# Moving splits, copies and one bank in a three-layer transformer kernel: four edits to the order of work on VectorE and ScalarE

## The chip, the cores and the metric

One core of a Trainium2 chip. The metric is the time on the device, in microseconds (us), of one execution of the whole program. The engines are called by the profile's names: PE is TensorE (PEld its weight loads), DVE is VectorE, ACT is ScalarE, POOL is GpSimd, SP is SyncE, which here only issues DMAs.

## The reference

For 256 tokens of width 2048, in fp32, three blocks follow each other. The first two are attention layers, the third is a mixer with a feed-forward net.

```python
# layer one (MLA): 16 heads, compressed queries and keys, rope on 64 dims, causal softmax
h = rmsnorm(x, layer_norm[0]); c_q, c_kv, k_rope, gate = split(h @ mla_w_in)
q = rmsnorm(c_q, q_norm) @ w_uq;  kv = rmsnorm(c_kv, kv_norm) @ w_ukv
x = x + (attention(q, kv, rope) * silu(gate)) @ mla_w_out
# layer two (SWA): 32 query heads, 4 key heads, window 128, a sink logit per head
q, k, v, gate = split(rmsnorm(x, layer_norm[1]) @ swa_w_in)
p = exp(s - m) / (sum(exp(s - m)) + exp(sink - m))
x = rmsnorm(x + (p @ v * silu(gate)) @ swa_w_out, final_norm)
# layer three: 8 attention heads with a relative bias beside a Mamba-2 mixer with 16 heads
q, k, v, z, xbc, dt = split(rms_norm(x, ln_mix_pre) @ w_in)
xbc = silu(causal_conv4(xbc));  dt = softplus(dt + dt_bias)
mixed = concat(softmax(q k / sqrt(128) + bias) @ v, gated_norm(ssd(xbc, dt), z)) @ w_out
x = x + rms_norm(mixed, ln_mix_post)
u = causal_conv3(rms_norm(x, ln_ffn_pre) @ w_ffn_up)
x = x + rms_norm((gelu(u_gate) * u_up) @ w_ffn_down, ln_ffn_post)
```

## The kernel before

All weights pass through PE once, 512 KB at a time, in "tiles" numbered through the whole program (`T_C`, `T_KR`, `T_MLA`, `T_MLAO`, `T_KV`, `T_SWA`, `T_SWAO`, `T_XBC`, `T_DT`, `T_MOBA`, `T_OUT`, `T_UP`, `T_DOWN`). A product of fp32 numbers is made from three matmuls: each operand is split into a high part (rounded to the type fp32r) and a low part (what the rounding left), and high x high, high x low and low x high are added up in PSUM. Activations come as such pairs too (`hTh`/`hTl`, `cTh`/`cTl`, `yTh`/`yTl`).

So each weight tile has four steps. SP loads it into one of 4 slots, once the low part of the tile 4 earlier is made (lines 414 to 422). ACT casts it to `w_high` (`split`, line 1171), once it has landed and PE is through with the tile 4 earlier. DVE makes `w_low` (`split`, line 1667). PE waits for the low part (`ready`) and does its matmuls: `block_b` (lines 506 to 508), 256 columns each with the weights loaded, or `block_a` (lines 514 to 516). On ACT and DVE the call `split(T + j)` works on tile `T + j + 3`, that is three tiles ahead (`LEAD = 3`).

There is no scheduler: the order on each engine is written out by hand. Between the splits stand the other steps of the layer, and every engine goes through its list in order, waiting on semaphores. `after(engine, sem, n)` waits until the semaphore has passed n. In the steps below `project` says that a step computes the next heads' projections, `attend` that it does the attention of the heads before.

- Layer one, start. `first_gate` computes the first gate tile by tile into bank 0, PE then computes the first queries into banks 0 and 1 in `mla_step(0, True, False)`. Before that it waits for `ml["gate"]`, which `gate_out(0)` on DVE (line 1844) gives when it has read bank 0. `gate_out` needs the tanh of `gate_tanh` on ACT (line 1308), before which a function table is loaded. `scores` is the name of banks 4 and 5; the shared rotary key was in bank 4.
- Layer two, `swa_step`. Five steps, the first without attention, the last (after the loop) with tiles of the out projection. Each attending step treats four head pairs m = 0 to 3: PE makes scores, DVE takes the maxima (line 1711) and their negatives (line 1732), ACT the exponentials (lines 1244, 1246) and that of the sink (line 1394), DVE adds it and scales the rows (`normalised`, lines 1740 to 1745), PE transposes them (line 544), ACT and DVE copy the two halves out (`pt0`, `pt1`, line 1751), PE multiplies with the values (`swa_values`), DVE gates the result (`out_`, line 1838) and POOL splits it (lines 2473, 2474). Sixteen weight tiles run between these. ACT also places the next queries (`qs`, line 1429), which need DVE's rope (lines 1995 to 1999).
- Layer three, before `moba_step`. `xbc_step` projects the input of the convolution and treats it one part late; the last part, `conv_begin(3, 0)` and so on, comes behind the tile `T_DT`. On DVE follow the dt chain (lines 2169 to 2175, with exponentials and a table load on ACT), the copy for the bias (line 2177), and then the first split of `moba_step`. In the first of those steps ACT also writes eight parts of the residual (line 1507) and copies the transposed rows out of PSUM (`xs_out`, line 1520), which PE's `ssm_cb` waits for.
- Layer three, the last `moba_step(4, False, True)`. PE goes through tiles of the out projection; DVE copies `pt1` behind tiles 2 and 3, and copies the attention rows from bank 7 (line 2286) behind tile 6; PE's `ssm_turned` needs bank 7 free for its last four transposes, and its tile 6 needs POOL's split of those rows.

Of the kernel before, what the change touches and what calls it, by code (L numbers as in the profile page):

```python
# [28 lines left out]
ACT = mybir.ActivationFunctionType  # L29
# [146 lines left out]
def after(eng, sem, count):  # L176

    eng.wait_ge(sem, count + 1)
# [23 lines left out]
def program(nc, a, out, toeplitz):  # L202
# [9 lines left out]
    with ctx:  # L212
# [283 lines left out]
        def _(pe):  # L496
# [137 lines left out]
            def first_gate(j):  # L634
                tile_b(T_MLA + j, [banks[0][:, 0:SEQ], banks[0][:, SEQ:2 * SEQ]], range(4 * j, 4 * j + 4), 256,
                       hTh, hTl, 0, DC - 1)
# [18 lines left out]
            def mla_step(i, project, attend):  # L655
# [21 lines left out]
                if project:  # L677
                    after(pe, ml["gate"], 1 if gated_first else i)
                    after(pe, ml["q_rope"], i)
# [478 lines left out]
        def _(act):  # L1158
# [145 lines left out]

            def gate_tanh(used):

                act.wait_ge(tiles_used, used)
                nc.scalar.activation(gtan[:, 0:2, :], banks[0].rearrange("p (h n) -> p h n", h=2), ACT.Tanh,
                                     scale=0.5).then_inc(ml["tanh"], 1)

            split(T_MLA + 2)
            split(T_MLA + 3)
            gate_tanh(T_MLA + 4)
            act.wait_ge(kr_done, 1)
# [69 lines left out]
            def swa_step(i, project, attend):  # L1384
                def tile(*js):

                    for j in js:
                        split(T_SWA + j, i, 16)
# [16 lines left out]
                if project:  # L1405
                    tile(1, 2, 3)
                    pt0(0)
                    tile(4)
                    exps(1)
                    tile(5)  # L1410
                    if not attend:
                        keys_placed()
                    tile(6, 7)
                    pt0(1)
                    tile(8)
                    act.wait_ge(tiles_used, T_SWA + 8 + i * 16)
                    after(act, sw["q_rope"], i)
                    for k in range(2):
                        last = nc.scalar.copy(qsr[:, 2 * k:2 * k + 2, :], banks[k].rearrange("p (h n) -> p h n", h=2))
                    last.then_inc(sw["q_out"], 1)  # L1420
                    exps(2)
                    tile(9, 10, 11)
                    pt0(2)
                    tile(12)
                    exps(3)

                    after(act, sw["s_ready"], 4 * i)
                    after(act, sw["q_rope"], i + 1)
                    nc.scalar.copy(qs[:, :, :], qs_next[:, :, :]).then_inc(sw["q_placed"], 1)
                    tile(13, 14, 15)  # L1430
                    pt0(3)
                    return
# [51 lines left out]
            split(T_DT)  # L1484
            conv_begin(3, 0)
            conv_tanh(3, 0)

            act.wait_ge(sm["dt_x"], 1)
# [5 lines left out]
            def moba_step(i, project, attend):  # L1494
                def tile(*js):

                    for j in js:
                        if project or j < 15:
                            split(T_MOBA + j, i, 16)
                        if project and not attend and j < 8:  # L1500
                            row_of_residual(j)
# [152 lines left out]
        def _(dve):  # L1654
# [184 lines left out]

            def gate_out(i):  # L1840

                after(dve, ml["tanh"], i + 1)
                after(dve, ml["y32_done"], i)
                v.scalar_tensor_tensor(gate[:, 0:2, :], gtan[:, 0:2, :], 1.0,
                                       banks[0].rearrange("p (h n) -> p h n", h=2),
                                       ALU.add, ALU.mult).then_inc(ml["gate"], 1)

            split(T_MLA + 2)
            split(T_MLA + 3)
            gate_out(0)  # L1850

# [112 lines left out]
            def swa_step(i, project, attend):  # L1964
# [56 lines left out]
                gates_in()  # L2021
                tile(1)
                norm(0)
                tile(2)
                if project and not attend:
                    keys_rope()
                if project:
                    gates_out()
                    tile(3)
                    pt1(0)  # L2030
                    tile(4)
                    maxima(1)
                    out_(0)
                    tile(5)
                    norm(1)
                    tile(6, 7)
                    pt1(1)
                    tile(8)
                    maxima(2)
                    out_(1)  # L2040
                    tile(9)
                    norm(2)
                    tile(10)
                    rope(0)
                    tile(11)
                    pt1(2)
                    rope(1)
                    tile(12)
                    maxima(3)
                    out_(2)  # L2050
                    tile(13)
                    norm(3)
                    tile(14, 15)
                    pt1(3)
                    out_(3)
                    return
# [3 lines left out]
                maxima(1)  # L2060
                tile(4)
                out_(0)
                norm(1)
                tile(5, 6)
                pt1(1)
                maxima(2)
                tile(7)
                out_(1)
                norm(2)
                tile(8, 9)  # L2070
                pt1(2)
                maxima(3)
                tile(10)
                out_(2)
                norm(3)
                tile(11, 12)
                pt1(3)
# [80 lines left out]
            with dve.Fori(1, 3) as i:  # L2158
                chain.enter(i - 1, 4)
                xbc_step(i)  # L2160
            chain.leave(2)
            split(T_DT)
            conv_input(3, 0)
            conv_taps(3, 0)
            conv_silu(3, 0)

            dve.wait_ge(tiles_used, T_DT + 1)
# [11 lines left out]
            def moba_step(i, project, attend):  # L2179
                def tile(*js):  # L2180

                    for j in js:
                        if project or j < 15:
                            split(T_MOBA + j, i, 16)
# [59 lines left out]
                if not project:  # L2244
# [6 lines left out]
                    last.then_inc(sm["gated"], 1)  # L2251
                tile(2, 3)
                if attend:
                    copy_pt1(mb, i - 1, sc[:, 0, 0:384])
                if project:
                    dve.wait_ge(tiles_used, T_MOBA + 4 + i * 16)
# [7 lines left out]
                if not project:  # L2264
                    dve.wait_ge(sm["rstd"], 1)
                    for g in range(SSM_G):
                        for t in range(TT):
                            cols = nx[:, t, g * 512:(g + 1) * 512]
                            last = v.tensor_scalar(cols, cols, rstd[:, 2 * g + t:2 * g + t + 1], None, ALU.mult)
                    last.then_inc(sm["yn"], 1)  # L2270
                tile(4, 5)
                if project and not attend:
# [7 lines left out]
                    dve.wait_ge(sm["acs"], 1)  # L2280
                select(0)
                tile(6)
                if attend:
                    after(dve, mb["o_ready"], i)
                    after(dve, mb["y_split"], i - 1)
                    v.tensor_copy(y32[:, :, :], banks[7].rearrange("p (h n) -> p h n", h=2)).then_inc(mb["y32_done"], 1)
                if project and not attend:
# [310 lines left out]
```

## Time and profile before

| | us |
|---|---|
| median of 3 runs | 1871.04 |
| lowest and highest | 1866.25, 1874.73 |
| the profiled execution | 1870.36 |
| its span in the trace | 1868.6 |
| DVE busy, ACT busy | 1146.0 (61%), 897.5 (48%) |
| DMA, mean over the span | 174 GB/s, HBM read 321 MB |
| mean granted clock of PE | 0.994 of full speed |

Times in the rows are us from the span's start, mean durations of groups are ns. A name on the left of `<-` is what is written. In brackets at a row's end stands how long the engine was idle before it and what ended that; "issue" is a wait for which the profile names no releaser. The end of a matmul's row is modelled, and rows of PE overlap.

### The profile page before, as it was taken

To read this page: it belongs to the slowest core of one execution; us is meant where nothing else is said; L and a number is where in the kernel's file an instruction comes from. 1 tells how busy PE (TensorE), PEld (TensorE's weight loads), DVE (VectorE), ACT (ScalarE), POOL (GpSimd) and SP (SyncE) were. 2 spreads that over 40 slices of the span, in tenths; PEclk is the share of its full clock that TensorE was granted. 3 is DMA by queue.
4 is the path that set the end of the run, shared out by engine and by line. 5 is a ranking of instruction groups with operands and counts; after the bars stand their busy time and mean duration, and the time that the engine had idled before them with its cause. 6 is when DMAs were issued, how large, how long until landed. Compare 5 with 4: busy or idle time off the path is not lost. (4 is left out here: it accounts for less than half of the span.)

```text
span 1868.6 us, 35194 instructions
## 1 busy us (share of the span) xinstructions
PE 1811.4 (97%) x13068; PEld 1681.9 (90%) x13068; DVE 1146.0 (61%) x1806; ACT 897.5 (48%) x1350; POOL 149.4 (8%) x180
## 2 busy tenths in 40 slices
PE   6999999999999899999999998999999999999998
PEld 5899998899888778999999788999999999988886
DVE  6555555656666666765665556666666666744445
ACT  6465554554444455454433444544544454443333
POOL 1001110000101101000000000100000000033331
PEclk9999999999999999999999999999999999999999
DMA  7555555565444456655555464656666666665554
GB/s 232 165 150 150 164 156 174 184 175 170 133 140 154 133 172 181 173 181 158 147 149 166 158 192 147 191 185 193 196 199 194 193 188 189 195 201 192 195 193 140
DMA packets 234940, 324.34 MB, mean 174 GB/s; under 512 B 12288, under 2 KB 170260, under 8 KB 234224
## 3 DMA queue, kind: packets, MB, share of 16 engines
q1 hardware_dynamic: 233440, 318.61, 55.4%
q0 software_dynamic: 1136, 4.58, 0.8%
q8 instruction: 52, 0.85, 0.2%
q14 instruction: 24, 0.20, 0.0%
q10 hardware_dynamic: 288, 0.11, 0.0%
HBM read 321.14 MB, written 2.11 MB: 173 GB/s over the span
## 5 line engine op out<-in xcount | busy, mean ns | idle before, releaser
L1667 DVE TENSOR_TENSOR w_low<-raw,w_high 128x1024 fp32r<-128x1024 f32 x603 | 736.2, 1230 | 619.4 <-ACT w_high L1171 617.6
L1171 ACT CAST w_high<-raw 128x1024 fp32r<-128x1024 f32 x603 | 626.7, 1049 | 665.0 <-PE bank L508 342.7
L506 PE MATMUL bank<-hT_high,w_high 128*128 128x256 f32 x2640 | 739.4, 280 | 8.1 <-DVE hT_low L1684 2.8
L507 PE MATMUL bank<-hT_low,w_high 128*128 128x256 f32 x2640 | 733.0, 278 | 0.0
L508 PE MATMUL bank<-hT_high,w_low 128*128 128x256 f32 x2640 | 732.9, 278 | 0.0
L506 PEld LDWEIGHTS bank<-hT_high,w_high 128*128 128x128 f32 x2640 | 498.2, 189 | 15.4 <-issue 6.2
L507 PEld LDWEIGHTS bank<-hT_low,w_high 128*128 128x128 f32 x2640 | 497.6, 188 | 0.1
L508 PEld LDWEIGHTS bank<-hT_high,w_low 128*128 128x128 f32 x2640 | 497.6, 188 | 0.0
L514 PE MATMUL bank<-w_high,yT_high 128*128 128x512 f32 x384 | 152.8, 398 | 3.8 <-issue 2.0
L515 PE MATMUL bank<-w_low,yT_high 128*128 128x512 f32 x384 | 150.4, 392 | 0.0
L516 PE MATMUL bank<-w_high,yT_low 128*128 128x512 f32 x384 | 150.4, 392 | 0.0
L1132 PE MATMUL bank<-w_high,hidden_low 128*128 128x512 f32 x264 | 102.7, 389 | 0.0
L1130 PE MATMUL bank<-w_high,hidden_high 128*128 128x512 f32 x264 | 102.7, 389 | 0.0
L1131 PE MATMUL bank<-w_low,hidden_high 128*128 128x512 f32 x264 | 102.7, 389 | 0.0
L514 PE MATMUL bank<-w_high,hT_high 128*128 128x256 f32 (+1 forms) x320 | 97.6, 305 | 0.0
L515 PE MATMUL bank<-w_low,hT_high 128*128 128x256 f32 (+1 forms) x320 | 96.3, 301 | 0.0
L516 PE MATMUL bank<-w_high,hT_low 128*128 128x256 f32 (+1 forms) x320 | 96.3, 301 | 0.0
L514 PEld LDWEIGHTS bank<-w_high,yT_high 128*128 128x128 f32 x384 | 72.4, 189 | 21.2 <-issue 4.0
L516 PEld LDWEIGHTS bank<-w_high,yT_low 128*128 128x128 f32 x384 | 72.5, 189 | 15.5
L515 PEld LDWEIGHTS bank<-w_low,yT_high 128*128 128x128 f32 x384 | 72.6, 189 | 14.7
L2473 POOL CAST yT_high<-y_rows 128x256 f32 (+3 forms) x28 | 16.4, 586 | 648.0 <-DVE y_rows L1838 466.1
L514 PEld LDWEIGHTS bank<-w_high,hT_high 128*128 128x128 f32 x320 | 60.1, 188 | 8.5 <-issue 6.1
(321 smaller groups left out, 2097.4 us busy)
## 6 DMA issues: line engine op xcount, KB each, us to landing
raw<-in_w_up SPq DMA_DIRECT2D x176, 512.0 KB, 4.4
raw<-in_w_in SPq DMA_DIRECT2D x88, 512.0 KB, 3.7
raw<-in_w_down SPq DMA_DIRECT2D x88, 512.0 KB, 4.5
raw<-in_w_swa SPq DMA_DIRECT2D x72, 512.0 KB, 3.7
raw<-in_w_c SPq DMA_DIRECT2D x50, 512.0 KB, 3.8
raw<-in_w_mlao SPq DMA_DIRECT2D x32, 512.0 KB, 3.7
raw<-in_w_swao SPq DMA_DIRECT2D x32, 512.0 KB, 3.9
raw<-in_w_out SPq DMA_DIRECT2D x32, 512.0 KB, 3.8
```

The costliest lines, as they stand in the source:

```text
L506: nc.tensor.matmul(to, h, act_h[:, chunk, :], start=first, stop=False, skip_group_check=True)
L507: nc.tensor.matmul(to, h, act_l[:, chunk, :], start=False, stop=False, skip_group_check=True)
L508: return nc.tensor.matmul(to, l, act_h[:, chunk, :], start=False, stop=last, skip_group_check=True)
L514: nc.tensor.matmul(to, ah, h, start=first, stop=False, skip_group_check=True)
L515: nc.tensor.matmul(to, ah, l, start=False, stop=False, skip_group_check=True)
L516: return nc.tensor.matmul(to, al, h, start=False, stop=last, skip_group_check=True)
L1130: nc.tensor.matmul(to, ah, wh[:, w], start=first, stop=False, skip_group_check=True)
L1131: nc.tensor.matmul(to, ah, wl[:, w], start=False, stop=False, skip_group_check=True)
L1132: last = nc.tensor.matmul(to, al, wh[:, w], start=False, stop=True, skip_group_check=True)
L1171: nc.scalar.copy(whi(tile, i, n), raw[s][:, :]).then_inc(high_made, 1)
L1667: v.tensor_tensor(wlo(tile, i, n), raw[s][:, :], whi(tile, i, n).bitcast(F32), ALU.subtract).then_inc(low_made, 1)
L2473: chain.done(g_.tensor_copy(h, y32[:, 0:n, :]))
```

## The change

Four edits. (1) `first_gate` writes bank 5 instead of bank 0, `gate_tanh` and `gate_out` read it there, and PE no longer waits for `ml["gate"]` in the first step. (2) In `swa_step` on DVE the scaling `norm(m)` comes ahead of the split or splits between it and the maxima (and in the last step `out_(m)` does too); on ACT split 13 comes ahead of the copy to `qs`. (3) In the last `moba_step` on DVE the copy of `pt1` comes between splits 2 and 3, and the rows copy (`rows_out`) ahead of split 6. (4) Splits `T_MOBA` and `T_MOBA + 1` are made within the last part of the convolution on both engines, instead of at the start of the first `moba_step`; on DVE `conv_input(3, 0)` goes ahead of `split(T_DT)`.

```diff
             def first_gate(j):
-                tile_b(T_MLA + j, [banks[0][:, 0:SEQ], banks[0][:, SEQ:2 * SEQ]], range(4 * j, 4 * j + 4), 256,
+                tile_b(T_MLA + j, [banks[5][:, 0:SEQ], banks[5][:, SEQ:2 * SEQ]], range(4 * j, 4 * j + 4), 256,
...
                 if project:
-                    after(pe, ml["gate"], 1 if gated_first else i)
+                    if not gated_first:
+                        after(pe, ml["gate"], i)
...
-            gate_tanh(T_MLA + 4)
+            gate_tanh(T_MLA + 4, banks[5])
...
                     exps(3)
-
+                    tile(13)
                     after(act, sw["s_ready"], 4 * i)
                     after(act, sw["q_rope"], i + 1)
                     nc.scalar.copy(qs[:, :, :], qs_next[:, :, :]).then_inc(sw["q_placed"], 1)
-                    tile(13, 14, 15)
+                    tile(14, 15)
...
             conv_begin(3, 0)
+            split(T_MOBA)
             conv_tanh(3, 0)
+            split(T_MOBA + 1)
...
-                        if project or j < 15:
+                        early = project and not attend and j < 2
+                        if (project or j < 15) and not early:
                             split(T_MOBA + j, i, 16)
...
-            gate_out(0)
+            gate_out(0, banks[5])
...
                 gates_in()
-                tile(1)
                 norm(0)
-                tile(2)
+                tile(1, 2)
...
                     out_(0)
-                    tile(5)
                     norm(1)
-                    tile(6, 7)
+                    tile(5, 6, 7)
...
                     out_(1)
-                    tile(9)
                     norm(2)
-                    tile(10)
+                    tile(9, 10)
                     rope(0)
...
                     out_(2)
-                    tile(13)
                     norm(3)
-                    tile(14, 15)
+                    tile(13, 14, 15)
...
                 maxima(1)
-                tile(4)
                 out_(0)
                 norm(1)
-                tile(5, 6)
+                tile(4, 5, 6)
...
+            conv_input(3, 0)
             split(T_DT)
-            conv_input(3, 0)
+            split(T_MOBA)
             conv_taps(3, 0)
             conv_silu(3, 0)
+            split(T_MOBA + 1)
...
-                tile(2, 3)
+                tile(2)
+                if project:
+                    tile(3)
                 if attend:
                     copy_pt1(mb, i - 1, sc[:, 0, 0:384])
+                if not project:
+                    tile(3)
...
+                def rows_out():
+
+                    after(dve, mb["o_ready"], i)
+                    after(dve, mb["y_split"], i - 1)
+                    v.tensor_copy(y32[:, :, :], banks[7].rearrange("p (h n) -> p h n", h=2)).then_inc(mb["y32_done"], 1)
...
                 select(0)
+                if not project:
+                    rows_out()
                 tile(6)
-                if attend:
-                    after(dve, mb["o_ready"], i)
-                    after(dve, mb["y_split"], i - 1)
-                    v.tensor_copy(y32[:, :, :], banks[7].rearrange("p (h n) -> p h n", h=2)).then_inc(mb["y32_done"], 1)
+                if project and attend:
+                    rows_out()
```

## Rows read from the trace of the kernel before

**Rows 1.** The page: engine, busy us (share of the span) and instructions.

```profile
PE 1811.4 (97%) x13068; PEld 1681.9 (90%) x13068; DVE 1146.0 (61%) x1806; ACT 897.5 (48%) x1350; POOL 149.4 (8%) x180
```

**Rows 2.** Waits of PE in 440 to 630 us: us in total, times, longest.

```profile
PE bank L544 <- DVE prob L1745: 11.9, 12, 2.4
```

**Rows 3.** Windows: length, busy us (instructions) of the five engines, PE's clock, DMA share, GB/s.

```profile
87.80:91.20 3.40, 3.40 (x19) 3.40 (x18) 0.44 (x1) 0.61 (x1) 0.00 (x0) 0.50 0.77 226
...
559.60:563.00 3.40, 3.40 (x29) 3.40 (x30) 2.53 (x3) 0.59 (x1) 0.00 (x0) 1.00 0.69 199
...
1053.80:1057.10 3.30, 3.30 (x9) 2.63 (x8) 0.23 (x1) 0.00 (x0) 0.00 (x0) 0.50 0.89 292
```

**Rows 4.** Timeline of PE, end of the first gate: start, us, line, operands.

```profile
83.06 0.28 PE L508 MATMUL bank<-hT_high,w_low 128*128 128x256 f32 x1
86.99 0.36 PE L506 MATMUL bank<-cT_high,w_high 128*128 128x256 f32 x1 [3.65 <-issue]
```

**Rows 5.** Timeline of DVE there.

```profile
83.25 2.35 DVE L1667 TENSOR_TENSOR w_low<-raw,w_high 128x1024 fp32r<-128x1024 f32 x2
86.08 0.69 DVE L1844 SCALAR_TENSOR_TENSOR gate<-gate_tanh,bank 128x512 f32<-128x512 f32 x1 [0.48 <-ACT gate_tanh L1308]
```

**Rows 6.** Timeline of PE, layer two, pairs 2 and 3 of one step, 3 of the next.

```profile
485.99 0.44 PE L541 MATMUL bank<-prob_T,v_swa_placed 128*64 128x256 f32 x2 [0.61 <-issue]
...
497.64 1.54 PE L544 MATMUL bank<-constants,prob 128*128 128x128 f32 x6 [2.41 <-DVE prob L1745]
...
559.58 0.87 PE L544 MATMUL bank<-constants,prob 128*128 128x128 f32 x6 [2.21 <-DVE prob L1745]
```

**Rows 7.** Timeline of DVE and ACT at pairs 2 and 3 of that step.

```profile
485.47 0.42 DVE L1751 COPY prob_T<-bank 128x256 f32<-128x256 f32 x1
...
495.02 1.23 DVE L1667 TENSOR_TENSOR w_low<-raw,w_high 128x1024 fp32r<-128x1024 f32 x1 [3.58 <-ACT w_high L1171]
...
497.23 0.35 DVE L1745 TENSOR_SCALAR prob<-prob,row_rcp 128x256 f32<-128x256 f32 x1
...
492.91 0.19 ACT L1394 ACTIVATE sink_exp<-sink_distance 128x4 f32<-128x4 f32 x1
...
493.95 2.93 ACT L1171 CAST w_high<-raw 128x1024 fp32r<-128x1024 f32 x3
```

**Rows 8.** Timeline: the last attention step (PE, DVE), then POOL alone and beside DVE.

```profile
1043.59 0.45 PE L541 MATMUL bank<-prob_T,v_moba 128*128 128x256 f32 x1 [1.08 <-issue]
...
1050.95 0.33 PE L544 MATMUL bank<-constants,nx 128*128 128x128 f32 x1 [1.75 <-DVE y_rows L2286]
...
1052.98 0.50 PE L514 MATMUL bank<-w_high,yT_high 128*128 128x512 f32 x1 [1.37 <-POOL yT_low L2474]
...
1040.66 2.36 DVE L1667 TENSOR_TENSOR w_low<-raw,w_high 128x1024 fp32r<-128x1024 f32 x2 [3.57 <-ACT w_high L1171]
...
1044.98 2.36 DVE L1667 TENSOR_TENSOR w_low<-raw,w_high 128x1024 fp32r<-128x1024 f32 x2
1049.07 1.23 DVE L1667 TENSOR_TENSOR w_low<-raw,w_high 128x1024 fp32r<-128x1024 f32 x1 [1.73 <-ACT w_high L1171]
1050.21 0.68 DVE L2286 COPY y_rows<-bank 128x512 f32<-128x512 f32 x1
...
461.08 0.40 POOL L2473 CAST yT_high<-y_rows 128x256 fp32r<-128x256 f32 x1 [61.88 <-DVE y_rows L1838]
...
626.33 1.22 DVE L1667 TENSOR_TENSOR w_low<-raw,w_high 128x1024 fp32r<-128x1024 f32 x1
...
626.58 1.22 POOL L2473 CAST yT_high<-y_rows 128x256 f32 x1 [11.42 <-DVE y_rows L1838]
```

**Rows 9.** Timeline of PE and ACT behind the last convolution.

```profile
815.78 0.38 PE L506 MATMUL bank<-hT_high,w_high 128*128 128x256 f32 x1 [2.00 <-DVE w_low L1667]
...
819.56 1.05 ACT L1171 CAST w_high<-raw 128x1024 fp32r<-128x1024 f32 x1 [0.71 <-DMA raw<-in_w_in]
...
821.14 1.18 ACT L1520 COPY gain_rows<-scores 128x256 f32<-128x256 f32 x4
```

More of the change, by code:

```diff
@@ L1303, in _, with gate_tanh @@
                 last.then_inc(c_hh, 1)
-            def gate_tanh(used):
+            def gate_tanh(used, bank=banks[0]):
                 act.wait_ge(tiles_used, used)
-                nc.scalar.activation(gtan[:, 0:2, :], banks[0].rearrange("p (h n) -> p h n", h=2), ACT.Tanh,
+                nc.scalar.activation(gtan[:, 0:2, :], bank.rearrange("p (h n) -> p h n", h=2), ACT.Tanh,
                                      scale=0.5).then_inc(ml["tanh"], 1)
@@ L1838, in gated, with gate_out @@
                 v.scalar_tensor_tensor(to, o, 0.5, g, ALU.mult, ALU.mult).then_inc(st["y32_done"], 1)
-            def gate_out(i):
+            def gate_out(i, bank=banks[0]):
                 after(dve, ml["tanh"], i + 1)
@@ L1844, in gate_out @@
                 v.scalar_tensor_tensor(gate[:, 0:2, :], gtan[:, 0:2, :], 1.0,
-                                       banks[0].rearrange("p (h n) -> p h n", h=2),
+                                       bank.rearrange("p (h n) -> p h n", h=2),
                                        ALU.add, ALU.mult).then_inc(ml["gate"], 1)
@@ L2060, in swa_step @@
                 maxima(1)
-                tile(4)
                 out_(0)
                 norm(1)
-                tile(5, 6)
+                tile(4, 5, 6)
                 pt1(1)
                 maxima(2)
-                tile(7)
                 out_(1)
                 norm(2)
-                tile(8, 9)
+                tile(7, 8, 9)
                 pt1(2)
                 maxima(3)
-                tile(10)
                 out_(2)
                 norm(3)
-                tile(11, 12)
+                tile(10, 11, 12)
                 pt1(3)
@@ L2182, in tile @@
                     for j in js:
-                        if project or j < 15:
+                        early = project and not attend and j < 2
+                        if (project or j < 15) and not early:
                             split(T_MOBA + j, i, 16)
```

## The prediction

> **What bounds the kernel now.** The page first: TensorE (PE) is busy 97% of the span [rows 1]. So only gaps in its stream, and stretches where it runs slower, can pay; a faster vector or scalar engine by itself pays nothing. A matmul of 256 columns is 0.28 us long in its row [rows 4] but 29 of them start in 3.40 us [rows 3], one every 0.117. Its row thus overlaps the next one's by 0.16, and a gap costs the idle time that the profile prints plus 0.16.
>
> The table of PE's waits, in the layer-two stretch, shows what ends the gaps: 12 waits of 11.9 us in all for the last scaling of `prob` (line 1745) [rows 2], three steps of four head pairs. The loss is 11.9 + 12 x 0.16 = 13.8 us. I then read PE alone in the timeline for the other gaps that the change touches [rows 4, 6, 8, 9], and the same windows on VectorE (DVE), ScalarE (ACT) and GpSimd (POOL) for what is late.
>
> Last, the windows with PE's clock. After some gaps PE is granted 0.50, the 1.2 GHz level, for 3.4 us: 19 matmuls start from 87.8 us where 29 start from 559.6 at 1.00 [rows 3]. That costs 3.4 / 2 = 1.7 us where it falls on matmuls only, about 1.5 where gaps lie in it. The stretches from 497.4 and 620.3 read like the one from 87.8; with 1053.8 that makes four behind gaps that the change touches. Length alone doesn't decide it: an idle time of 2.41 us was followed by the lower clock, one of 2.21 at 559.58 was not [rows 3, 6].
>
> **First gate in bank 5.** PE starts the query tiles at 86.99 after 3.65 us idle [rows 4]. It waited for `gate_out(0)`, whose DVE row ends at 86.77 [rows 5] and frees bank 0. With the gate in bank 5 that wait is dropped, and PE can start at 83.2. What is next: the low halves of the following two tiles are the two splits from 83.25 [rows 5], ready at 84.4 and 85.6. PE needs the first only after one tile of 18 matmuls, at 85.3, and the second at 87.4. The tile after that is split right behind `gate_out`, by 88.3, and is needed at 90.1. So nothing takes the place of the wait: -3.65 - 0.16 = -3.8 us. Bank 5 is also the second score bank, first written by PE at the next step, some 7 us after `gate_out` has read it; the ACT and DVE work behind it there is in order, so no cost. The low clock that followed goes too (counted below).
>
> **Scaling ahead of the split, layer two.** At pair 3 of a step the sink's exponential ends on ACT at 493.10, but DVE first waits for ACT's next cast, which stands behind the copy of `qs` and starts at 493.95, splits at 495.02 and scales until 497.58; PE, idle 2.41, goes at 497.64 [rows 6, 7]. After the change the scaling starts at 493.15 and lasts 1.41 (its first operation starts where the split's 1.15 us are over, 496.17, its last ends at 497.58), so it ends at 494.6. PE's own work before it ends at 497.64 - 2.57 = 495.07. The gap is gone, with 0.45 to spare. Pairs 0 to 2 have more spare. All 12 waits go: -13.8 us.
>
> What is late next is the transposed copy on DVE (`pt1`). At pair 2 PE idles 0.61 for it (start 485.99) [rows 6]; the copy stood behind the rope and a split [rows 7]. DVE now comes to the rope some 0.9 earlier, because it no longer waits between scaling and two splits, while PE comes 0.4 earlier. Of the 0.77 about 0.3 stays: -0.5 x 3 steps = -1.5. At pair 3 three splits' time changes: casts 13, copy of `qs`, casts 14 and 15 end on ACT near 496.9, the two last splits on DVE near 498.35, the copy at 498.7, PE at 498.75: +0.05 x 3, bounds 0 to +0.6 each. The splits that move back (by at most 1.3 us) are of a tile that PE wants three tiles, 8 us, later; their loads by SP go out as much later and have as much room. In the last step, which has no such wait in [rows 2], I take nothing. Sum of the part: -15.2, bounds -13 to -15.5.
>
> **The last attention step, layer three.** DVE copies `pt1` behind two splits [rows 8]; PE idles 1.08 for it. One split fewer brings it 1.15 earlier. The rows copy, now ahead of split 6, no longer waits for ACT's cast: it follows the splits at 1044.98 to 1047.34, so it starts at 1047.26 instead of 1050.21, 2.95 earlier. It frees bank 7 for PE (idle 1.75) and starts POOL's split, for which PE idles 1.37 more [rows 8]. PE gets its 12 flips of the other banks done in the meantime. From PE's flip at 1050.95 to its tile at 1052.98 are 2.03 us, POOL's path. Undisturbed, the tile starts at 1050.05: -2.9.
>
> But the rows show a price. POOL's cast of 256 columns takes 0.40 alone and 1.22 beside a DVE split, ending 0.26 after it [rows 8]. Before, POOL worked beside scalings out of PSUM; now it starts at 1048.02 beside split 6, which runs about 1047.9 to 1049.1 since its cast waits for PE. I take 1.0 us for that, bounds 0 and 1.2: -1.9, bounds -1.7 to -2.9.
>
> The Trainium skill, SBUF — State Buffer (Who interferes with whom), says that a DVE instruction with two SBUF inputs and a GpSimd instruction that reads SBUF exclude each other, the second to issue waiting out the first. The 1.22 against 0.40 agree. By it the part gives -1.9; without it -2.9 and a total 1 us lower. It speaks against putting the rows copy right ahead of a split.
>
> **Two splits inside the last convolution.** PE idles 2.00 at 815.78 for a low half, which DVE makes only after the whole dt chain [rows 9]. Made earlier, it is there by 807. But both splits and the wait for a free slot now lie in front of the dt chain, which I put 3.2 us later (two splits of 1.15 and 0.9 of waiting). ACT then does the residual rows and the copies `xs_out`, on which PE's `ssm_cb` waits; they started at 821.14 [rows 9]. They move by +3.2, less two casts of 0.95 done already, less the 0.71 for which ACT waited on a DMA that now goes out early: +0.6. PE comes to `ssm_cb` 2.2 earlier and waits there. So the gap is not removed but moved; about 0.1 to 0.3 is left, and 0.4 from the second `xs_out` that no longer waits for a late cast. I take -0.6, bounds +0.6 to -2.2. POOL's load of the bias goes out 3 us later, and is wanted 30 us later.
>
> **The lower clock.** The four stretches cost 1.7 + 1.5 + 1.5 + 1.7 = 6.4 us, and their gaps go or shrink. Three gaps of 2 to 2.5 us stay or arise (PE's wait for POOL at the start of the last step of layer two, `ssm_cb`, POOL in the last attention step); of the like in rows 6, some were followed by the low clock, some not. I count one that comes: +1.6. Net -4.8, bounds -6.4 to -1.6.
>
> The Trainium skill, TensorE: Matmul & The Clock Gate (Part 1), calls the number of slow matmuls run-variable. This trace alone can't show that; it would widen the range and leave the sum.
>
> **The sum.** -3.8 - 15.2 - 1.9 - 0.6 - 4.8 = -26.3 us. The profiled execution took 1870.4, so 1844.1; it is 0.7 under the median of the runs shown, so 1844.5 to 1845. I say 1844.5. The rest of the kernel moves rigidly: every load waits for a slot that PE's progress frees.
>
> **The rivals.** (1) The gaps move on. The new last waits (`pt1`, weights, POOL) take back a third or more of the 21.5 us of gaps and the low clock returns at three places: -14 - 1.6, 1855, range 1851 to 1861. For it: two of the parts do just that. Against it: the spare times above. Chance 0.15. (2) The change doesn't do what it says: what PE waits for at the pairs isn't the order on DVE but something that ends with it. Then only gate and last step pay, 5.7 + 3.4 of clock: 1862, or no change at all if the profile's releasers mislead. Against it: the scaling's rows follow the split without a pause in all reads. Chance 0.05. (3) Slower: the scaling now holds the split behind it until ACT's exponentials are through, 2.0 + 1.4 us in each of 12 pairs. It decides once the lead of three tiles, 8 us, is used up, and PE then waits for low halves: 12 x 3.4 = +41 less 26, 1885. Nothing in the rows has DVE so far behind; at pair 3 the split is even made earlier, 494.5 for 495.02. Chance 0.03. (4) Everything falls well: no low clock returns and `ssm_cb` doesn't wait, under 1837. Chance 0.05. My forecast, 1838 to 1851, has 0.72.
>
> **Chances.** A measurement here can tell about 0.5%, 9 us, from no change. Faster by more: 0.72 + 0.05 + 0.13 of (1) = 0.90; within: 0.06; slower: 0.04. Range 1837 to 1854.
>
> **What would show it.** Line 1745 gone from PE's waits; PE's query tiles at 83.2; about 1.7 us of `pt1` waits; a new PE wait for `xs_out` near 800 of 2 us; POOL's last cast over 1 us long. I am wrong if PE waits for line 1667 inside the pairs, or if the clock is at 0.50 in more than three stretches between 80 and 1130 us.

## The result, and the profile after

The changed kernel takes 1843.31 us (median of 4 runs, 1842.34 to 1843.97); the kernel before, run beside it, 1871.65 (4 runs, 1866.25 to 1874.73). The ratio is 0.9853, with a 95% interval of 0.9835 to 0.9871. Forecast were 1844.5 and a range of 1837 to 1854. The ratios here and below are not quite the quotients of the medians; one run of the kernel before, taken beside the first experiments, took 3685.94 us and stands in none of them. The profiled execution took 1843.97, 26.4 us less than the one of before; so did its span, 1842.2 for 1868.6.

The page answers to [rows 1]: the span and the busy time of the engines.

```profile
span 1842.2 us, 35194 instructions
...
PE 1804.2 (98%) x13068; PEld 1677.8 (91%) x13068; DVE 1146.3 (62%) x1806; ACT 895.7 (49%) x1350; POOL 150.3 (8%) x180
```

The instructions are the same in number and DVE's busy time is too. PE is busy 7.2 us less while the span is 26.4 us shorter. So 19.2 us of the gain is idle time. The rest is clock, and the 0.16 us for each closed gap by which a row overlaps the next.

PE's waits after, over the whole span (us in total, times, longest); the first is the wait for the first DMAs at the start.

```profile
PE bank L620 <- DMA vector_rows<-in_ssm_norm: 12.6, 1, 12.6
PE bank L514 <- POOL yT_low L2484: 2.8, 2, 2.4
...
PE bank L514 <- issue: 2.0, 1, 2.0
PE scores L541 <- ACT gain_rows L1524: 1.8, 1, 1.8
...
PE bank L541 <- issue: 0.5, 3, 0.2
```

The 12 waits for the scaling [rows 2] are gone. Of the waits that the change touches, what is left is POOL's split in the last step of layer three (2.4), `xs_out` (1.8), and 0.5 for `pt1`. The 2.0 of line 514 is POOL's split in the last step of layer two, which the change leaves as it is.

To see where the time came from, each of the 13068 matmuls is taken by its number in PE's order, and its start after is subtracted from its start before. A positive shift means earlier. Apart from small steps of 0.1 us or less, it grows or falls only where a gap or a stretch of low clock differs:

| place (us of before) | shift | gained there | forecast |
|---|---|---|---|
| first gate's last tile, 83 | -0.28 | | |
| behind the query tiles' first, 84 | 3.54 | 3.82 | 3.8 |
| behind the low clock, 120 to 440 | 5.48 | 1.94, of it 0.2 in small steps | 1.7 |
| behind layer two, 625 to 812 | 23.81 | 18.33 | 15.2 + 1.5 + 1.5 |
| behind PE's wait at 815.8 | 26.09 | +2.3 | |
| behind `ssm_cb`, 829 to 1040 | 24.40 | -2.05, then +0.36 at the second pair of copies; in all 0.59 | 0.6 |
| behind the last attention step, 1058 | 26.36 | 1.96 | 1.9 + 1.7 - 1.6 |
| the end | 26.40 | | |

The matmuls that this rests on, in PE's timeline of after: the query tiles, pair 2 and pair 3 of layer two, and the two gaps that remain. They answer to [rows 4, 6, 8, 9].

```profile
83.33 0.28 PE L508 MATMUL scores<-hT_high,w_low 128*128 128x256 f32 x1
83.45 0.28 PE L506 MATMUL bank<-cT_high,w_high 128*128 128x256 f32 x1
...
477.41 0.44 PE L541 MATMUL bank<-prob_T,v_swa_placed 128*64 128x256 f32 x2 [0.18 <-issue]
...
486.58 0.28 PE L508 MATMUL bank<-hT_high,w_low 128*128 128x256 f32 x1
486.69 0.27 PE L544 MATMUL bank<-constants,prob 128*128 128x128 f32 x1
...
799.04 0.48 PE L541 MATMUL scores<-xbc_T 128*128 128x256 f32 x1 [1.78 <-ACT gain_rows L1524]
...
1026.63 0.55 PE L514 MATMUL bank<-w_high,yT_high 128*128 128x512 f32 x1 [2.38 <-POOL yT_low L2484]
```

Where PE idled 3.65 and 2.41 us, the next matmul now starts 0.12 and 0.11 behind the last one, at its normal pace.

DVE at pair 3 after, to be read against [rows 7]: the scaling is over at 486.05 and the split comes behind it.

```profile
485.70 0.35 DVE L1749 TENSOR_SCALAR prob<-prob,row_rcp 128x256 f32<-128x256 f32 x1
485.97 1.22 DVE L1671 TENSOR_TENSOR w_low<-raw,w_high 128x1024 fp32r<-128x1024 f32 x1
487.39 2.36 DVE L1671 TENSOR_TENSOR w_low<-raw,w_high 128x1024 fp32r<-128x1024 f32 x2 [0.21 <-ACT w_high L1172]
489.67 0.42 DVE L1755 COPY prob_T<-bank 128x256 f32<-128x256 f32 x1
```

PE starts these transposes at 486.69, so the scaling, done at 486.05, is there 0.64 us early; the forecast had 0.45.

The windows of after (columns as in [rows 3]): the old places of the low clock at the queries and at pair 3, then the two places where it still is.

```profile
83.40:86.80 3.40, 3.40 (x32) 3.40 (x32) 2.92 (x4) 3.37 (x5) 0.00 (x0) 1.00 0.05 17
486.70:490.10 3.40, 3.40 (x32) 3.40 (x30) 3.18 (x4) 2.08 (x3) 0.00 (x0) 1.00 0.43 126
1027.00:1030.40 3.40, 3.40 (x10) 2.64 (x9) 0.89 (x3) 0.00 (x0) 0.17 (x1) 0.51 0.83 301
1119.20:1122.50 3.30, 3.30 (x18) 3.30 (x17) 2.95 (x6) 1.85 (x5) 0.00 (x0) 0.50 0.67 207
```

Before the last microseconds of the span, five stretches of some 3.4 us at 0.50 (from 87.8, 497.4, 620.3, 1053.7 and 1145.9) have become two.

### The profile page after: what moved, and what is told of

It reads as the page before. It is cut to its first block and busy times, and to the rows that moved or that the text cites. A ratio compares the mean times of both kernels' runs of the same rounds, so it can differ in the third digit from the quotient of the medians.

```text
span 1842.2 us, 35194 instructions
## 1 busy us (share of the span) xinstructions
PE 1804.2 (98%) x13068; PEld 1677.8 (91%) x13068; DVE 1146.3 (62%) x1806; ACT 895.7 (49%) x1350; POOL 150.3 (8%) x180
## 5 line engine op out<-in xcount | busy, mean ns | idle before, releaser
L506 PE MATMUL bank<-hT_high,w_high 128*128 128x256 f32 x2608 | 729.8, 280 | 6.0 <-DVE hT_low L1688 2.7
L508 PE MATMUL bank<-hT_high,w_low 128*128 128x256 f32 x2608 | 724.0, 278 | 0.0
L507 PE MATMUL bank<-hT_low,w_high 128*128 128x256 f32 x2608 | 723.9, 278 | 0.0
L506 PEld LDWEIGHTS bank<-hT_high,w_high 128*128 128x128 f32 x2608 | 491.3, 188 | 13.1 <-issue 5.8
L508 PEld LDWEIGHTS bank<-hT_high,w_low 128*128 128x128 f32 x2608 | 490.7, 188 | 0.0
L507 PEld LDWEIGHTS bank<-hT_low,w_high 128*128 128x128 f32 x2608 | 490.6, 188 | 0.1
```

The source lines that it names most:

```text
L506: nc.tensor.matmul(to, h, act_h[:, chunk, :], start=first, stop=False, skip_group_check=True)
L507: nc.tensor.matmul(to, h, act_l[:, chunk, :], start=False, stop=False, skip_group_check=True)
L508: return nc.tensor.matmul(to, l, act_h[:, chunk, :], start=False, stop=last, skip_group_check=True)
```

## The experiments

The theory: four independent gaps on PE were closed, 3.8 + 15.2 + 1.9 + 0.6 us, and fewer gaps left fewer stretches at the lower clock. The rivals: the gaps only move on, some edit does nothing and another does its work, or the time comes from something that the edits share, such as the clock. First each edit was made alone on the kernel before.

**Edit 1 alone** (gate in bank 5).

```diff
-                tile_b(T_MLA + j, [banks[0][:, 0:SEQ], banks[0][:, SEQ:2 * SEQ]], range(4 * j, 4 * j + 4), 256,
+                tile_b(T_MLA + j, [banks[5][:, 0:SEQ], banks[5][:, SEQ:2 * SEQ]], range(4 * j, 4 * j + 4), 256,
...
-                    after(pe, ml["gate"], 1 if gated_first else i)
+                    if not gated_first:
+                        after(pe, ml["gate"], i)
...
```

> The kernel before with edit 1 alone: first gate in bank 5, no wait for ml[gate] in the first step. Theory (each edit takes out its own gap and the low clock behind it, and they add up): PE starts the query tiles near 83.4 us instead of 86.99, the clock stays at 1.00 there, everything behind it is 5.3 to 5.8 us earlier, time near 1866, with four stretches of low clock left. Rival (the edits help each other, and a gain up front is given back where layer two waits): the start is as early, but the gaps of layer two grow and the end is under 3 us earlier.

Measured: 1864.8 (10 runs, 1860.95 to 1869.27), ratio 0.9975 (0.9963 to 0.9988). The shift goes from -0.07 to 3.74 at the queries, is 5.34 at 95 and stays there to 497: 5.4 us, the gap and its stretch of low clock, as forecast. PE's waits in layer two (430 to 630 us) are in number and place those of before:

```profile
PE bank L544 <- DVE prob L1746: 11.4, 12, 2.4
PE bank L514 <- issue: 2.0, 1, 2.0
PE bank L541 <- issue: 1.8, 3, 0.6
```

But the shift ends at 8.50, not 5.4. Nothing in the code behind 95 us differs, and the gaps are the same; still the low clock is elsewhere. Four windows of this kernel: behind the gap of each of the three pairs 3, and at the last attention step.

```profile
492.20:495.60 3.40, 3.29 (x28) 3.30 (x29) 2.65 (x4) 0.59 (x1) 0.00 (x0) 1.00 0.74 189
552.70:556.10 3.40, 3.28 (x16) 3.29 (x17) 2.66 (x4) 0.59 (x1) 0.00 (x0) 0.50 0.80 190
614.60:618.00 3.40, 3.37 (x29) 3.37 (x30) 2.58 (x3) 0.59 (x1) 0.00 (x0) 1.00 0.75 228
1046.90:1050.30 3.40, 3.40 (x16) 2.81 (x15) 0.27 (x2) 1.05 (x1) 0.00 (x0) 1.00 0.90 292
```

The three pair-3 gaps here cost 2.37, 2.37 and 2.56 us (idle 2.21, 2.21 and 2.40); only the middle one was followed by 0.50. So the size of a gap does not decide it, and one profiled execution does not say what another will do. Single runs bear this out. Here are all ten of edit 1 and the 18 of the kernel before beside them, by their mean granted clock:

| mean granted clock | edit 1 alone, us | before, same chip, us |
|---|---|---|
| 0.997 | 1860.95, 1861.87 | |
| 0.996 | 1862.66, 1864.14, 1864.28 | |
| 0.995 | 1865.31 | 5 runs, 1867.86 to 1869.53 |
| 0.994 | | 9 runs, 1869.79 to 1872.23 |
| 0.993 | 1868.02, 1868.86, 1869.07, 1869.27 | 1871.92, 1872.05, 1872.27, 1872.91 |

At one and the same clock, 0.993, the four runs of each kernel have means of 1868.8 and 1872.3: 3.5 us apart, about the gap. Within either kernel a lower clock in the main goes with a longer time, and between the fastest and the slowest run of edit 1 lie 8.3 us for 0.004 of the clock. So most of the spread of these two kernels is the clock.

**Edit 2 alone** (layer two, both engines) and **without its ScalarE line**. On DVE each `norm` goes ahead of the split before it, as in the diff of the change; on ACT:

```diff
+                    tile(13)
                     after(act, sw["s_ready"], 4 * i)
...
-                    tile(13, 14, 15)
+                    tile(14, 15)
```

> The kernel before with edit 2 alone: scaling ahead of the splits on VectorE, split 13 ahead of the copy to qs on ScalarE. Theory: no PE wait for line 1745 is left, 15.2 us of gaps and about 3 us of low clock go, time near 1853.5. Rival (edits depend on each other): under 12 us.

> As e2, but without its line on ScalarE: split 13 stays behind the copy to qs. Theory (the order on VectorE does it all; ScalarE comes to the end of copy and casts at the same time either way): within 0.6 us of e2, and the scaling of pair 3 ends as early as in e2. Rival (ScalarE's cast 13 was the late one, since VectorE's split waited 3.6 us for it): 2 us or more of the gap at each of the three pairs 3 stays, 6 us slower than e2.

Measured: 1851.8 (4 runs, 1850.84 to 1853.38), ratio 0.9903 (0.9887 to 0.992); without the ACT line 1854.39 (4 runs, 1852.72 to 1854.88), ratio 0.9917 (0.9901 to 0.9934). The shift over layer two is 18.25 and 18.29. So edit 2 makes all of the 18.3 that the full change shows there, by itself, and the order on DVE alone does it. Both executions lose 1.6 us of it again at once, to a stretch at 0.50 that starts at 610.91 and at 611.40, behind the wait for POOL that the edit leaves as it is; they get it back at the last attention step, where before has such a stretch and they have none. Without the ACT line pair 3 reads so on DVE; it waits 0.40 for the cast, and PE doesn't wait for anything here:

```profile
491.64 0.35 DVE L1745 TENSOR_SCALAR prob<-prob,row_rcp 128x256 f32<-128x256 f32 x1
492.39 3.50 DVE L1667 TENSOR_TENSOR w_low<-raw,w_high 128x1024 fp32r<-128x1024 f32 x3 [0.40 <-ACT w_high L1171]
495.80 0.42 DVE L1751 COPY prob_T<-bank 128x256 f32<-128x256 f32 x1
```

The ACT line thus gains nothing in the trace. The medians differ by 2.6 us, but the intervals of the two ratios overlap and the low clock differs from run to run; whether the line is worth anything is left open.

**Edit 3 alone** (last attention step).

```diff
-                tile(2, 3)
+                tile(2)
+                if project:
+                    tile(3)
                 if attend:
                     copy_pt1(mb, i - 1, sc[:, 0, 0:384])
+                if not project:
+                    tile(3)
...
+                def rows_out():
...
                 select(0)
+                if not project:
+                    rows_out()
                 tile(6)
...
```

> The kernel before with edit 3 alone, the last attention step of layer three. Theory: POOL's cast of the rows starts beside VectorE's split 6 and takes 1.5 to 1.7 us instead of 0.6, and ends 0.3 to 0.5 us behind the split; PE's tile starts 1.9 to 2.0 us earlier, against 2.9 if nothing were in POOL's way; the low clock behind it may stay. Time near 1869.5. Rival (POOL isn't slowed by the split): cast 0.6 us, tile 2.9 us earlier.

Measured: 1869.12 (10 runs, 1867.33 to 1870.95), ratio 0.9991 (0.9981 to 1.0001). The time alone can't tell 2 us from nothing; the trace can. The shift over the step is 2.2 (from -2.54 to -0.37), with one stretch of low clock in both kernels. DVE and POOL:

```profile
1050.47 1.23 DVE L1667 TENSOR_TENSOR w_low<-raw,w_high 128x1024 fp32r<-128x1024 f32 x1
...
1050.53 1.64 POOL L2483 CAST yT_high<-y_rows 128x512 fp32r<-128x512 f32 x1 [6.91 <-DVE y_rows L2279]
1052.25 1.27 POOL L2484 TENSOR_TENSOR yT_low<-y_rows,yT_high 128x512 fp32r<-128x512 f32 x1
```

The cast starts 0.06 behind the split, runs beside it and ends 0.47 behind it. This profiled execution has seven stretches of low clock where before's has five, and is as long for that reason.

**Edit 4 alone** (splits within the convolution; the lines of ACT are shown, those of DVE are as in the diff of the change).

```diff
             conv_begin(3, 0)
+            split(T_MOBA)
             conv_tanh(3, 0)
+            split(T_MOBA + 1)
...
```

> The kernel before with edit 4 alone, two splits inside the last convolution. Theory (the gap moves on: ScalarE comes to the copies xs_out 0.3 to 0.6 us earlier only): PE's 2.0 us wait for the low half is gone, a wait of about 1.8 us for xs_out stands ahead of ssm_cb, everything behind is 0.5 to 0.7 us earlier; time 1870.5, not to be told from before. Rival (the two splits pay alone): 2 us.

Measured: 1869.83 (10 runs, 1867.43 to 1871.62), ratio 0.9997 (0.9986 to 1.0007). PE's wait for the low half at 815.78 [rows 9] is gone, and the only wait between 780 and 830 us is a new one:

```profile
PE scores L541 <- ACT gain_rows L1523: 1.8, 1, 1.8
...
823.41 0.48 PE L541 MATMUL scores<-xbc_T 128*128 128x256 f32 x1 [1.79 <-ACT gain_rows L1523]
```

The shift goes from -0.54 to 1.73 and back to 0.12 at 829: the gap was moved, for 0.66 us net.

The four ratios say together 0.25 + 0.97 + 0.09 + 0.03 = 1.34% of the 1.47% of the full change, well within their intervals; the quotients of the medians say 1.54% of 1.51%. In the traces the four parts, each read over its own stretch, are 5.4, 18.25, 2.2 and 0.66 us, in all 26.5, where the full change shows 26.40 + 0.28 from its first matmuls to the end. So no help or hindrance between the edits shows.

Next, the prices that the prediction put on what was left.

**Split 6 later**: the changed kernel, with split 6 of the last step behind the four low parts of the mixer's rows, so that no split runs beside POOL's cast. It tests the 1.0 us.

```diff
                 if not project:
                     rows_out()
-                tile(6)
+                if project:
+                    tile(6)
...
                         last.then_inc(sm["y_low"], 1)
+                    tile(6)
```

> The kernel after, but in the last attention step VectorE makes split 6 behind the low parts of the mixer's rows, so that it doesn't run beside POOL's cast of the attention rows. Theory (the two instructions exclude each other): POOL's cast takes 0.6 us instead of 1.6, PE's tile starts 1.0 us earlier, its idle time before falls to 1.5 us or less; where a low clock followed it, that goes too; time 1.0 to 2.7 us under the kernel after. Rival (the cast is slow for another reason): no change, or slower by a wait for the late low half of tile 9.

Measured: 1841.39 (4 runs, 1840.85 to 1841.8), ratio to before 0.985 (0.9831 to 0.987). POOL and PE in the timeline, then the window behind them (columns as in [rows 3]):

```profile
1024.03 0.61 POOL L2485 CAST yT_high<-y_rows 128x512 fp32r<-128x512 f32 x1 [6.91 <-DVE y_rows L2279]
1024.71 1.27 POOL L2486 TENSOR_TENSOR yT_low<-y_rows,yT_high 128x512 fp32r<-128x512 f32 x1
...
1026.04 0.50 PE L514 MATMUL bank<-w_high,yT_high 128*128 128x512 f32 x1 [1.36 <-POOL yT_low L2486]
```

```profile
1026.10:1029.50 3.40, 3.40 (x15) 2.83 (x16) 2.94 (x6) 1.10 (x4) 0.48 (x1) 1.00 0.95 314
```

The same cast takes 0.61 where it took 1.63 in the changed kernel. In the kernel before it took 0.61 too, beside scalings on DVE that read PSUM:

```profile
1050.96 0.61 POOL L2473 CAST yT_high<-y_rows 128x512 fp32r<-128x512 f32 x1 [9.88 <-DVE y_rows L2286]
```

So it is the split and not a busy DVE that slows it. 1.02 us is what the split beside it costs, and PE's tile starts 1.02 us earlier against its surroundings. Here the lower clock did not follow, which is worth another 1.6: the shift goes from -0.43 to 2.18.

**`xs_out` earlier**: the changed kernel with the first two copies behind one cast on ACT instead of three. It tests whether ACT's order holds PE at `ssm_cb`.

```diff
-                tile(2, 3)
+                tile(2)
+                if project and not attend:
+                    xs_out(0, 1)
+                tile(3)
                 if attend:
                     copy_pt0(mb, i - 1)
                 tile(4)
-                if project and not attend:
-                    xs_out(0, 1)
...
```

> The kernel after, but ScalarE makes the first two copies xs_out behind one cast of the first step of layer three instead of behind three. Theory (what is late for ssm_cb is only the order on ScalarE): PE's wait of 1.8 us for xs_out goes, everything behind 1.9 to 2.2 us earlier, 1841 to 1841.5. Rival (the wait moves on to the second pair of copies, the load of the bias or a low half): under 0.7 us.

Measured: 1841.72 (4 runs, 1839.71 to 1842.89), ratio to before 0.9855 (0.9835 to 0.9875). No wait of PE between 780 and 810 is left, and the shift against the changed kernel grows there by 2.05 (0.61 to 2.66), the gap of 1.95 and a little. It is the whole of what edit 4 had moved. Here too no stretch at 0.50 follows in the last attention step, though PE's gap of 2.37 us idle for POOL is still there; that is another 1.6.

**Maxima first**: the changed kernel with `maxima(0)` ahead of split 0 in the last step of layer two, where POOL splits beside a DVE split in the same way [rows 8].

```diff
-                tile(0)
+                if project:
+                    tile(0)
                 maxima(0)
+                if not project:
+                    tile(0)
                 gates_in()
```

> The kernel after, but in the last step of layer two VectorE takes the maxima ahead of the first split, so that the split doesn't run beside POOL's cast of the last pair. Theory (exclusion, as in n1): the cast takes 0.4 us instead of 1.2, PE's wait for POOL falls from 2.0 to 1.2 us idle, everything behind 0.8 us earlier. Rival: no change.

Measured: 1844.71 (4 runs, 1841.89 to 1845.25), ratio to before 0.9864 (0.9843 to 0.9885), so no faster than the changed kernel. The gap did shrink:

```profile
603.27 0.40 POOL L2486 CAST yT_high<-y_rows 128x256 f32 x1 [7.36 <-DVE y_rows L1842]
...
604.65 0.47 PE L514 MATMUL bank<-w_high,yT_high 128*128 128x512 f32 x1 [1.16 <-issue]
```

The window behind the gap of `xs_out`, further on in the same kernel:

```profile
799.60:802.90 3.30, 3.30 (x16) 3.12 (x15) 3.11 (x9) 1.68 (x6) 0.00 (x0) 0.50 0.96 297
```

The cast is 0.40 for 1.22, PE idles 1.16 for 1.99, and the shift grows by 0.84 at this matmul. But behind the unchanged gap of `xs_out` this profiled execution has a stretch at 0.50 that the changed kernel's does not, and loses 1.6 us by it. A gain of 0.8 us is under what the clock's place does to one run.

**The scaling twice**: the changed kernel with a second set of the four scalings in front of each set in layer two, into tiles that nobody reads there (0.9 us more on DVE, 16 times; the output stays the same). It measures the spare times.

```diff
+                for h in range(2 if sink else 0):
+                    v.tensor_scalar(kraw[:, h, 0:P], prob[:, h, 0:P], rc[:, 0, h:h + 1], None, ALU.mult)
+                    v.tensor_scalar(krot[:, h, :], prob[:, h, P:384], rc[:, 1, h:h + 1], None, ALU.mult)
```

> The kernel after with the four scalings of each head pair of layer two issued twice, the first time into tiles that nobody reads any more: 0.9 us more on VectorE in each of 16 pairs, nothing else. It measures the spare time that the prediction gave. Theory: at pairs 0 and 1 nothing, at pair 3 the spare time is 0.45 us so that PE idles 0.4 to 0.5 us, and at pair 2 the copy pt1 comes 0.9 later: 3 x (0.45 + 0.9) = 4 us later behind layer two. Rival A (the splits behind the scaling decide, PE waits for low halves): waits for w_low in the pairs, 10 us or more. Rival B (there is much more spare time): under 1.5 us.

Measured: 1849.04 (4 runs, 1848.15 to 1852.4), ratio to before 0.989 (0.9873 to 0.9907). PE's waits in 430 to 610 us:

```profile
PE bank L541 <- issue: 3.3, 3, 1.1
PE bank L514 <- issue: 2.0, 1, 2.0
PE bank L544 <- DVE prob L1752: 0.9, 3, 0.4
```

At pair 2 the gap for `pt1` grows from 0.35 to 1.28, by all of the 0.9; at pair 3 the scaling now comes 0.33 to 0.52 too late, so 0.4 to 0.6 of the 0.9 was spare (0.45 forecast). Pairs 0 and 1 show nothing and PE never waits for a low half. So the scaling is what PE waits for as soon as the spare time is used up, and at pair 2 `pt1` at once: from 440 to 625 us the shift falls by 6.0, of which some 1.6 is a low clock from 609, and 4.4 the gaps.

**All together**: the changed kernel with the last step, `xs_out` and maxima edits above, and at pair 2 of layer two `pt1(2)` ahead of split 11.

```diff
                     rope(0)
-                    tile(11)
                     pt1(2)
+                    tile(11)
```

> The kernel after with the changes of the three runs before (split 6 behind the low parts, xs_out behind one cast, maxima first in the last step of layer two) and a fourth: at pair 2 VectorE copies pt1 ahead of split 11 instead of behind it. Theory (the gaps add up, and no gap over 2 us is left between 100 and 1090 us): -1.0 - 1.9 - 0.7 - 3 x 0.25 = -4.4 us of gaps, and the low clock seen at 1027 us goes, -1.6: time near 1837.3, less spread than before. Rival (gains at one place are taken back at the next by waits or by another low clock): 1840 or more.

Measured: 1838.42 (5 runs, 1837.79 to 1839.66), ratio to before 0.9829 (0.9816 to 0.9843): 4.9 us under the changed kernel, with intervals that just overlap. The page of waits has 1.2 left of the 2.0 in the last step of layer two and 1.4 of the 2.4 in that of layer three:

```profile
PE bank L514 <- POOL yT_low L2490: 1.8, 2, 1.4
...
PE bank L514 <- issue: 1.2, 1, 1.2
```

The shift against the changed kernel grows by 0.8 at 605, 2.05 at 799, 1.0 at 1026 and 1.6 of clock behind that. The earlier `pt1` closes its three gaps, which gains 0.25 us or a little more each time, but small steps between them give back more than half of it: over the loop the shift grows by 0.3.

## Why the prediction was right

**The first gate.** Right. -3.8 forecast, 3.82 in the shift. PE's query tiles start at 83.45 instead of 83.2; that is the start of the kernel, which came 0.28 later in this execution.

**Layer two.** Right in place and size. All 12 waits went, 18.3 us with the clock for 15.2 + 3.0. Of `pt1` about 0.35 us of gap is left at each of three pairs 2 (idle 0.18) where 0.3 was forecast. The one line that doesn't hold is among the signs: "about 1.7 us of `pt1` waits" does not follow from the working, which leaves three times 0.3. The trace shows 0.5 of idle time, 1.0 with the overlap. The spare time at pair 3 was found by the doubled scaling, not only argued. The ACT line was taken as a part of it without need: the runs give it no share in the trace.

**The last attention step.** Right: PE's tile starts 1.95 earlier against its surroundings, for 1.9. The 1.0 us for POOL beside split 6 was a choice between bounds of 0 and 1.2; the cast took 1.63 beside the split and 0.61 without it, 1.02. The rule that the prediction names beside this term, of the Trainium skill, SBUF — State Buffer (Who interferes with whom), held here: the cast started 0.07 behind the DVE split, which has two SBUF operands, and ended 0.47 behind it. Moving the split gave the time back, so this is shown by a run and not by a likeness of rows.

**The convolution.** Right: 0.59 for 0.6, and by its terms: 0.23 is left of the gap and 0.36 comes from the second pair of copies, where 0.1 to 0.3 and 0.4 were forecast. The new wait for `xs_out` is at 799.04 with 1.78 us, as "near 800 of 2 us". That ACT's queue, not the splits, holds it was shown by moving the copies ahead of two casts, which gave 2.05 us.

**The clock.** The sum came out as forecast, four stretches gone and one back, 1.6 us, and at a place that was named. But the forecast took the stretches of one profiled execution as belonging to their gaps, and the runs show that they do not: with edit 1 alone, two stretches of layer two and the one at the last step were missing behind gaps that had not changed, and one appeared elsewhere. Four traces still have the three gaps at pairs 3 (before, and edits 1, 3 and 4 alone): 7 of these 12 gaps were followed by a stretch at 0.50, seldom the longer ones (one of four with 2.40 or 2.41 us idle, six of eight with 2.21). The term of -4.8 was an average that happened to be met; the bounds of -6.4 to -1.6 were the honest part. The Trainium skill, TensorE: Matmul & The Clock Gate (Part 1), calls the number of slow matmuls in the warm-up run-variable. Of the stretches behind gaps, which are another place, the runs here show the same: a mean clock of 0.993 to 0.997 over 10 runs of edit 1 alone.

**The rivals.** Gaps that move on: one did, `xs_out`, and it was in the forecast; elsewhere nothing came. That the change doesn't do what it says is refuted by edit 2 alone. Splits held back so far that PE waits for low halves: not even with 0.9 us more in front of each. A time under 1837 would have needed the gaps that stayed to go as well; with them shortened or closed the kernel still takes 1838.4.

## What to carry to other kernels

Where one engine is busy 97% of the span, list its gaps by what ends them, add to each the overlap of its rows, and ask of each what stands in the helper's queue ahead of the step that it waits for and is itself needed only later. Here weight splits wanted three tiles later stood ahead of scalings wanted at once, and swapping them cost nothing; where the cause is the length of a queue (ACT before `xs_out`), making two items earlier only moves the gap until the awaited copy itself goes forward. Judge an edit of 1 or 2 us by the start times of the same matmul in two traces, since its effect on the total is drowned by where the low clock happens to fall.

## What the runs showed of the hardware

- A stretch at 0.50 cost 1.5 to 1.7 us where it fell, and it comes and goes behind one and the same gap. Over all the traces here, the gap of 3.65 us idle at the queries was followed by it in 5 of 5, those of 2.21 to 2.41 at pairs 3 in 7 of 12, and that of 1.99 in the last step of layer two in 4 of 10. The gap of some 1.79 at `xs_out` was followed by it in 1 of 5 (maxima first), that of some 2.38 for POOL in the last attention step in 4 of 5.
- Whether fewer gaps also mean less spread from run to run is not shown. The 4 runs of the changed kernel lie within 1.6 us and the 5 of all edits together within 1.9, but 4 of maxima first lie within 3.4, and of the kernels with 10 runs the one with edit 1 alone has the widest spread, 8.3.
- POOL's cast of 512 columns takes 0.61 us where DVE is idle or scales out of PSUM, and 1.63 beside a DVE split; that of 256 columns takes 0.40 and 1.22. On DVE's side the split shows nothing of it (1.23 beside the cast, mean 1.229 over all 603).
